# One transformer block and one recurrent/expert block on one core: weight pieces split in pairs, the second mixer in rounds of six column groups, the top-k decode over more pieces

## What is computed

```python
# first block
h = rmsnorm(x, pre_mix_gain);  proj = h @ w_in                # 2048 x 6144
o = 8 heads stick-breaking attention, 8 heads dilated attention with rope, each head normalised
x = x + rmsnorm(o @ w_out)
x = x + rmsnorm(conv_geglu(rmsnorm(x) @ w_up) @ w_down)       # width 5504
# second block
z = rms_norm(x) @ w_in2        # four parts of 1024: xr, gr, gu, gv
xc = depthwise conv of 4 taps over xr
for each direction:            # forward and backward
    a = exp(-8 softplus(-lam) sigmoid(xc @ w_a)); u = sqrt(1 - a*a) * sigmoid(xc @ w_x) * xc
    h_dir = scan(a, u)
a_out = gelu(gr) * (h_forward + h_backward)
b_out = gelu(gu) * (w_s @ layer_norm(gelu(gv)) + b_s)
x = x + concat(a_out, b_out) @ w_out2
# experts: 8 heads, top 16 of 128 + 128 keys, then the top 16 of the 256 sums, of 16384 experts
q = rms_norm(x) @ w_q;  ids, g = topk(topk(q0 @ keys0) + topk(q1 @ keys1))
x = x + (gelu(xn @ expert_u[ids]) * g) @ expert_v[ids]
out = rms_norm(x, final_gain)
```

## Time and profile before

| | us |
|---|---|
| three runs | 3196.59, 3196.71, 3199.45 |
| profiled execution | 3196.1 |
| its span | 3194.8 |
| PE busy | 3073.6 (96%) |
| DVE busy | 2115.2 (66%) |
| ACT busy | 1724.6 (54%) |
| POOL busy | 617.6 (19%) |
| mean granted clock of PE | 0.986 |
| read from HBM | 553.99 MB, 174 GB/s |

### The profile page before, as it was taken

How to read it: one execution, slowest core, us unless ns; L and a number is a source line. 1 busy time by engine, 2 the same in 40 slices (tenths; PEclk the granted TensorE clock), 3 DMA queues, 4 the chain that set the end, 5 groups by cost and what they waited for, 6 DMA issues and landing times.

```text
span 3194.8 us, 52641 instructions
## 1 busy us (share of the span) xinstructions
PE 3073.6 (96%) x21302; PEld 2813.3 (88%) x21302; DVE 2115.2 (66%) x3523; ACT 1724.6 (54%) x3249; POOL 617.6 (19%) x528
## 2 busy tenths in 40 slices
PE   7999989999999999889998999999999999999998
PEld 6999879999998877888897998889998888999886
DVE  5565566666665556665799997557777556777655
ACT  5588755555554445675454544454444454444444
POOL 0011001111110001340233445002326001224200
PEclk9999999999999999999998999999999999999999
DMA  6434435555556554436443445554444555444553
GB/s 243 177 138 146 172 135 184 183 185 185 185 182 216 196 185 178 147 139 222 145 169 137 161 170 176 192 186 172 172 172 172 186 193 175 172 171 173 188 192 135
DMA packets 79875, 559.49 MB, mean 175 GB/s; under 512 B 9361, under 2 KB 10641, under 8 KB 12689
## 3 DMA queue, kind: packets, MB, share of 16 engines
q1 hardware_dynamic: 79632, 556.12, 49.2%
HBM read 553.99 MB, written 2.10 MB: 174 GB/s over the span
## 4 chain that ended last, share of the span: by engine, by line
PE 79%; DVE 4%; ACT 2%; issue 1%; POOL 1%; ACTq 0%; POOLq 0%; DVEq 0%
PE ps L243 14%; PE ps L244 14%; PE ps L245 14%; PE ps L254 12%; PE ps L256 12%; PE ps L255 12%; PE ps L1083 1%; DVE loR L226 1%; PE ps L685 1%; ACT hiR L219 0%; ACT fo L375 0%; DVE lX L783 0%; DVE x L1462 0%; DVE tmp L273 0%; DVE eq L1028 0%
## 5 line engine op out<-in xcount | busy, mean ns | idle before, releaser
L226 DVE TENSOR_TENSOR loR<-raw,hiR 128x512 fp32r<-128x512 f32 x1816 | 1334.5, 739 | 996.2 <-ACT hiR L219 992.8
L219 ACT CAST hiR<-raw 128x512 fp32r<-128x512 f32 x2052 | 1258.5, 619 | 912.7 <-PE ps L256 603.6
L243 PE MATMUL ps<-XAh,hiR 128*128 128x256 f32 x4192 | 1214.1, 290 | 3.1 <-DVE x L1462 2.6
L244 PE MATMUL ps<-XAl,hiR 128*128 128x256 f32 x4192 | 1186.7, 283 | 0.0
L245 PE MATMUL ps<-XAh,loR 128*128 128x256 f32 x4192 | 1186.2, 283 | 0.0
L243 PEld LDWEIGHTS ps<-XAh,hiR 128*128 128x128 f32 x4192 | 804.5, 192 | 6.4 <-DVE x L1462 3.1
L244 PEld LDWEIGHTS ps<-XAl,hiR 128*128 128x128 f32 x4192 | 804.9, 192 | 2.6 <-issue 1.9
L245 PEld LDWEIGHTS ps<-XAh,loR 128*128 128x128 f32 x4192 | 804.4, 192 | 0.0
L226 POOL TENSOR_TENSOR loR<-raw,hiR 128x512 fp32r<-128x512 f32 x236 | 322.5, 1366 | 1413.2 <-ACT hiR L219 1413.2
L254 PE MATMUL ps<-hiR,ah 128*128 128x512 f32 x1024 | 405.2, 396 | 6.2 <-DVE al L1114 6.2
L255 PE MATMUL ps<-loR,ah 128*128 128x512 f32 x1024 | 405.0, 395 | 0.0
(11 more groups left out here) (256 smaller groups left out, 3171.6 us busy)
## 6 DMA issues: line engine op xcount, KB each, us to landing
raw<-in_u_dram SPq DMA_DIRECT2D x128, 1024.0 KB, 4.8
raw<-in_v_dram SPq DMA_DIRECT2D x128, 1024.0 KB, 4.8
raw<-in_w_up_dram SPq DMA_DIRECT2D x86, 1024.0 KB, 4.8
raw<-in_w_down_dram SPq DMA_DIRECT2D x43, 1024.0 KB, 4.8
raw<-in_w_in_qk_dram SPq DMA_DIRECT2D x32, 1024.0 KB, 4.7
raw<-in_w_out_dram SPq DMA_DIRECT2D x32, 1024.0 KB, 4.8
raw<-in_w_in_dram SPq DMA_DIRECT2D x24, 1024.0 KB, 4.8
raw<-in_w_in_v_dram SPq DMA_DIRECT2D x16, 1024.0 KB, 4.8
```

What stands on the lines that cost most here:

```text
L219: e.copy(hiR[:, g % NQ, :], raw[n % NR][:, g % 4, :]).then_inc(S("hi"), 1)
L226: e.tensor_tensor(loR[:, g % NQ, :], raw[g // 4 % NR][:, g % 4, :], hiR[:, g % NQ, :].bitcast(F32), ALU.subtract).then_inc(S("lo_pool" if ...
L243: e.matmul(dst, wh, X.h[:, k, :], start=(k == 0), stop=False)
L244: e.matmul(dst, wh, X.l[:, k, :], start=False, stop=False)
```

## The change

`split_hi` and `split_lo` handle two pieces (128x1024) in one instruction, at even steps only, and wait until both ring places are free; `on_pool` now counts pairs. The second mixer's 24 column groups come in four rounds of six (`xr`, `gr`, `xr`, `gr`, `gu`, `gu`), 24 steps a round, so that the spatial gating of two chunks runs inside each round, in bank 3; the groups share banks 0 to 2. The gate matmuls move from step 20 to 22 of the round, and what follows them by two steps as well. `w_out2` is consumed in the order `WO2_ORDER`. `TKP` becomes 8, `DEC0` 76, the two decodes start 14 steps apart and PE transposes behind their step 13; the gates start at step 106.

The diff, cut to its core:

```diff
+WO2_ORDER = [0, 1, 2, 3, 4, 5, 8, 9, 10, 11, 12, 13, 14, 15, 6, 7]
...
-def on_pool(g):
+def on_pool(u):
+    g = 2 * u
     if P_IN <= g < P_WO2:
-        return g % 6 == 0
+        return u % 6 == 0
     if P_Q <= g < P_U[0]:
...
-            d, p = LO_COUNT[4 * (n - NR) + 3]
+            d, p = LO_COUNT[2 * (n - NR) + 1]
...
     def split_hi(e, g):
-        if g >= NP:
+        if g >= NP or g % 2:
             return
-        n = g // 4
-        if g % 4 == 0:
+        n, r, q = g // 4, g % NQ, g % 4
+        if q == 0:
             e.wait_ge(S(f"raw{n % NR}"), 16 * (n // NR + 1))
         if g >= NQ:
-            e.wait_ge(S("piece"), g - NQ + 1)
-        e.copy(hiR[:, g % NQ, :], raw[n % NR][:, g % 4, :]).then_inc(S("hi"), 1)
+            e.wait_ge(S("piece"), g - NQ + 2)
+        e.copy(hiR[:, r:r + 2, :], raw[n % NR][:, q:q + 2, :]).then_inc(S("hi"), 1)
...
-        if g >= NP or on_pool(g) != pool:
+        if g >= NP or g % 2 or on_pool(g // 2) != pool:
             return
-        e.wait_ge(S("hi"), g + 1)
-        e.tensor_tensor(loR[:, g % NQ, :], raw[g // 4 % NR][:, g % 4, :], hiR[:, g % NQ, :].bitcast(F32),
+        n, r, q = g // 4, g % NQ, g % 4
+        e.wait_ge(S("hi"), g // 2 + 1)
+        e.tensor_tensor(loR[:, r:r + 2, :], raw[n % NR][:, q:q + 2, :], hiR[:, r:r + 2, :].bitcast(F32),
                         ALU.subtract).then_inc(S("lo_pool" if pool else "lo_dve"), 1)
...
     def pe_mixer(e, s):
-        p, d = divmod(s - 20, 16)
+        p, d = divmod(s - 22, 24)
         if d == 0 and 0 <= p < 4:
...
-        c, d = divmod(s - 69, 4)
-        if d == 0 and 0 <= c < 8:
-            b = 4 + c % 2
+        p, d = divmod(s - 21, 24)
+        if d in (0, 4) and 0 <= p < 4:
+            c = 2 * p + d // 4
...
-                e.wait_ge(S("sig"), 32)
-            elif c >= 2:
-                e.wait_ge(S("gm_add"), c - 1)
+            else:
+                e.wait_ge(S("gm_add"), c)
             for tb in range(2):
...
         if d == 0 and 0 <= j < 24:
+            p, v = divmod(j, 6)
             e.wait_ge(S("piece"), P_IN + 4 * j + 4)
-            if j >= 16:
-                e.activation(guT[:, j - 16, :], bank[j % 4][:, 0:T], ACT.Gelu_apprx_tanh).then_inc(S("inev"), 1)
-            elif j % 2:
...
+        p, d = divmod(s - 16, 24)
         if d == 0 and 0 <= p < 4:
             for i in range(2):
                 c = 2 * p + i
-                e.wait_ge(S("inev"), 4 * p + 1 + 2 * i)
...
-            d = s - 16 * p
-            if d == 21:
+            d = s - 24 * p
+            if d == 23:
...
-            elif d == 22:
-                e.wait_ge(S("lam"), 21)
+            elif d == 24:
...
-            elif d == 23:
+            elif d == 25:
...
-            elif d == 24:
...
+            elif d == 26:
...
-            elif d == 26:
+            elif d == 28:
...
-        c, d = divmod(s - 73, 4)
-        if d == 0 and 0 <= c < 8:
+        p, d = divmod(s - 25, 24)
+        if d in (0, 4) and 0 <= p < 4:
+            c = 2 * p + d // 4
             e.wait_ge(S("gm_mul"), c + 1)
             e.copy(XA.h[:, 8 + c, :], gm[c % 2][:, :]).then_inc(S("gm_hi"), 1)
...
-            elif d == 24:
+            elif d == 26:
...
-            elif d in (26, 27):
-                i = d - 26
+            elif d in (28, 29):
+                i = d - 28
...
-        c, d = divmod(s - 70, 4)
-        if d == 0 and 0 <= c < 8:
+        p, d = divmod(s - 22, 24)
+        if d in (0, 4) and 0 <= p < 4:
+            c = 2 * p + d // 4
...
-            elif d in (27, 28):
-                i, c = d - 27, 2 * p + d - 27
+            elif d in (29, 30):
+                i, c = d - 29, 2 * p + d - 29
                 e.wait_ge(S("scan"), 2 * c + 2)
...
-            elif d in (29, 30):
-                c = 2 * p + d - 29
+            elif d in (31, 32):
+                c = 2 * p + d - 31
...
             e.tensor_tensor(gm[c % 2][:, :], gm[c % 2][:, :], guT[:, c, :], ALU.mult).then_inc(S("gm_mul"), 1)
-        c, d = divmod(s - 73, 4)
-        if d == 0 and 0 <= c < 8:
+        p, d = divmod(s - 25, 24)
+        if d in (0, 4) and 0 <= p < 4:
+            c = 2 * p + d // 4
...
-    TK0, TKP = 10, 9
+    TK0, TKP = 10, 8
     DEC0 = TK0 + 8 * TKP + 2
+    DECP = 14
...
-            if s - (DEC0 + 11 * tb) == 10:
+            if s - (DEC0 + DECP * tb) == 13:
...
-            d = s - (DEC0 + 11 * tb)
+            d = s - (DEC0 + DECP * tb)
...
-            elif d == 11:
+            elif d == 14:
...
     def dve_choice(e, s):
-        h, d = divmod(s - TK0, TKP)
         lo8, hi8 = slice(0, 8), slice(8, 16)
         chains = [(0, 0), (0, 1), (1, 0), (1, 1)]
-        if 0 <= h < 8:
+        for h in range(8):
...
+            elif d == 9:
...
-    GATE0 = [DEC0 + 24 - 4 * 16, 1, 1]
+    GATE0 = [DEC0 + 2 * DECP + 2 - 4 * 16, 1, 1]
...
         for j in range(24):
-            if j < 4:
+            if j < 3:
                 e.wait_ge(S("gv"), 2 if j < 2 else 4)
             else:
-                e.wait_ge(S("inev"), j - 3)
+                e.wait_ge(S("inev"), j - 2)
...
-            for k in range(KC):
+            for n, k in enumerate(WO2_ORDER):
                 if fb == 0:
                     e.wait_ge(S("l_lo" if k < 8 else "gm_lo"), k % 8 + 1)
-                moving(e, P_WO2 + 16 * fb + k, XA.h[:, k, :], XA.l[:, k, :], [bank[b][:, :] for b in pair], k == 0,
-                       k == KC - 1)
-                pe_mixer(e, 96 + 16 * fb + k)
+                elif fb == 1 and n == 0:
+                    e.wait_ge(S("gm_add"), 8)
+                moving(e, P_WO2 + 16 * fb + n, XA.h[:, k, :], XA.l[:, k, :], [bank[b][:, :] for b in pair], n == 0,
...
-                if n == P_IN // 4 + 4 * p + 10:
+                if n == P_IN // 4 + 6 * p + 10:
...
-    a["w_out2"] = _mov(I["w_out_2"][0])
+    blocks = []
+    for p in range(4):
+        for c in (2 * p, 2 * p + 1):
+            blocks += [w_in2[:, h * 1024 + c * 128:h * 1024 + (c + 1) * 128] for h in range(2)]
+        blocks += [w_in2[:, 2048 + c * 128:2048 + (c + 1) * 128] for c in (2 * p, 2 * p + 1)]
+    a["w_in2"] = _stat(np.concatenate(blocks, 1))
+    a["w_out2"] = _mov(I["w_out_2"][0], [(fb, k) for fb in range(4) for k in WO2_ORDER])
```

More of the change, by code:

```diff
@@ L50 @@
 NT = NP // 4
-def on_pool(g):
+def on_pool(u):
+    g = 2 * u
     if P_IN <= g < P_WO2:
-        return g % 6 == 0
+        return u % 6 == 0
     if P_Q <= g < P_U[0]:
-        return g % 3 == 0
+        return u % 3 == 0
     for r in range(3):
         if P_U[r] <= g < P_VV[r]:
-            return g % (2 if r == 0 else 3) == 0
+            return u % (2 if r == 0 else 3) == 0
     return False
 LO_COUNT, _n = [], {True: 0, False: 0}
-for _g in range(NP):
-    _n[on_pool(_g)] += 1
+for _u in range(NP // 2):
+    _n[on_pool(_u)] += 1
     LO_COUNT.append((_n[False], _n[True]))
@@ L693, in pe_mixer @@
                 e.wait_ge(S("mix_const"), 64)
-                e.wait_ge(S("sig"), 32)
-            elif c >= 2:
-                e.wait_ge(S("gm_add"), c - 1)
+            else:
+                e.wait_ge(S("gm_add"), c)
             for tb in range(2):
-                m = e.matmul(bank[b][:, half(tb)], gv[:, tb, c * 128:(c + 1) * 128], wsT[:, c, :], start=True,
+                m = e.matmul(bank[3][:, half(tb)], gv[:, tb, c * 128:(c + 1) * 128], wsT[:, c, :], start=True,
                              stop=True)
@@ L704, in act_mixer @@
         if d == 0 and 0 <= j < 24:
+            p, v = divmod(j, 6)
             e.wait_ge(S("piece"), P_IN + 4 * j + 4)
-            if j >= 16:
-                e.activation(guT[:, j - 16, :], bank[j % 4][:, 0:T], ACT.Gelu_apprx_tanh).then_inc(S("inev"), 1)
-            elif j % 2:
-                e.copy(grT[:, j // 2, :], bank[j % 4][:, 0:T]).then_inc(S("inev"), 1)
+            if v >= 4:
+                e.activation(guT[:, 2 * p + v - 4, :], bank[j % 3][:, 0:T], ACT.Gelu_apprx_tanh).then_inc(S("inev"), 1)
+            elif v % 2:
+                e.copy(grT[:, 2 * p + v // 2, :], bank[j % 3][:, 0:T]).then_inc(S("inev"), 1)
             else:
@@ L712, in act_mixer @@
                     e.wait_ge(S("xpz"), 16)
-                e.copy(xp[j // 2][:, 2:258], bank[j % 4][:, 0:T]).then_inc(S("inev"), 1)
-        p, d = divmod(s - 16, 16)
+                e.copy(xp[2 * p + v // 2][:, 2:258], bank[j % 3][:, 0:T]).then_inc(S("inev"), 1)
+        p, d = divmod(s - 16, 24)
         if d == 0 and 0 <= p < 4:
@@ L814, in pool_mixer @@
         for p in range(4):
-            d = s - 16 * p
-            if d == 22:
+            d = s - 24 * p
+            if d == 24:
                 for i in range(2):
@@ L1246, in act_program @@
         e.activation(tmp0[:, 0, :], x[:, 0, :], ACT.Square, accum_out=ss[:, 0:1]).then_inc(S("x0sq"), 1)
-        for g in range(2):
-            split_hi(e, g)
+        split_hi(e, 0)
         e.wait_ge(S("x0sq"), 1)
@@ L1252, in act_program @@
         act_root(e, 0, ss)
-        for g in range(2, 4):
-            split_hi(e, g)
+        split_hi(e, 2)
```

(12 more changed lines are left out.)

56 lines of the change are left out of this document (30 added, 26 removed).

## The result

The changed kernel takes **3211.62 us**, median of six runs (3208.80 to 3215.13); beside them the kernel before took 3197.74 (six runs, 3196.59 to 3199.45). The ratio is 1.0044, with a 95% interval of 1.0031 to 1.0057: slower by 14 us, and by more than the 0.2% that this kernel's measurement can tell. The forecast was 3193.0 within 3171 to 3207, so the result lies outside the range, on the side of rival B. The profiled execution has a span of 3211.5 us, 16.7 more than before.

A forecast was written before the change was run, and what follows sets the result against it. TensorE (PE) was taken as the bound, busy 3073.6 of 3194.8 us, so only its waits and lost clock could move: +8.5 + 2 + 5.4 - 8 - 11 - 0.6 = -3.7, forecast 3193.0 us, range 3171 to 3207.

The forecast's parts named there:

- rival B: Dilated heads: the seven longer waits for `tdl` also cost PE's clock, 1.7 us each, +12, total 3205; chance 0.17.
- Pair splits, price: All stages: a pair takes ACT 1.0 us to its result, DVE 1.14, POOL 2.4; 0.1 saved per pair on each engine.
- Heads: Dilated heads: PE gets `tdl` 1.2 us later, seven times, +8.5 us.
- Rounds: Second mixer: 30.4 us of waits and clock go, new waits of 12.6 and 2.3 and clock of 7.5 come: -8.
- A: Second mixer's rounds: POOL's pair is in time, so 12.6 and 7.5 fall away, total 3173; chance 0.25.
- C: Under the gates: DVE becomes the bound if a POOL pair takes 2.8 us, +7, total 3200; chance 0.10.
- E: Pair splits: pairs are no shorter than two single instructions, total 3196; chance 0.05.
- D: ACT's table switches: a further 1.38 us of drain with each load, by the page, total 3199; chance 0.03.
- Other hand-overs of a head: Dilated heads: hand-overs besides `tdl` lose up to the same but have about that much cover; +2 us.
- Stage borders: Borders at `w_out`, `w_out2` and the ends of `v`: pairs delay evacuations and sums by 0.8 to 1.0 each, together +5.4.
- Top-k and decode: First `fl` wait about 5 us, second decode's wait about 1: -11; gates begin two steps sooner, -0.6.
- The 10.4 us of clock in the old rounds: Second mixer before the change: rounds at 0.92 of full clock over 130 us, 10.4 lost, counted as gain to be had.

The follow-up runs named there:

- longer-wait kernels: The kernel before plus one unused DVE reduction ahead of the rotation in dilated heads 1 to 7, in three lengths (480, 1024, 2048): 3201.17, 3207.39, 3219.34 us.
- e3: The kernel before with only the top-k and decode constants changed (eight steps a head, 14 between the decodes), single splits: 3190.33 us, ratio 0.9979.
- e6: The changed kernel with LA = 5 instead of 6, so that pairs are split at odd steps: 3190.22 us, ratio 0.9977 to the kernel before.

## Why the prediction was wrong, and where it was right

**Right, step by step.** *Pair splits, price*: a cast pair took 1.03 to 1.06 (1.0 to its result forecast), DVE's 1.22 (1.14 to the follower), POOL's 2.34 (2.4). *Worth nothing in a steady stretch*: from 620 to 940 us, `w_up`, where pairs take 20 us off ACT's casts, the stage is 495.4 in both:

```profile
L225 ACT CAST hiR<-raw 128x1024 fp32r<-128x1024 f32 x112 | 117.3, 1047 | 154.3 <-PE ps L252 154.3
```

```profile
L219 ACT CAST hiR<-raw 128x512 fp32r<-128x512 f32 x223 | 137.3, 616 | 63.1 <-PE ps L245 63.1
```

The first line is the changed kernel's, the second the old one's; what ACT saves it adds to its wait for PE. *Heads*: `tdl` 15.2 (near 17), at the place named. *Rounds*: the chain to POOL's pair, and 3.3 three times (4.2); A, the pair in time, is out. C, DVE as the bound under the gates, is out too: under the gates no wait for DVE's `loR` appears, though a gate's product beside a POOL pair now takes 2.60, 0.52 alone, while 1.59 was its blocked time before: DVE stands as long as the pair runs, and there are half as many pairs. The sum over many gates stays (1557 ns a product between 1800 and 1900 us, 1592 before). The product, and POOL's pair beside it, which ends at 1804.86, 0.4 before the product does:

```profile
1802.64 2.60 DVE L1080 TENSOR_TENSOR OG<-OI,selb 128x344 f16<-128x344 f16 x1
1802.40 2.46 POOL L233 TENSOR_TENSOR loR<-raw,hiR 128x1024 fp32r<-128x1024 f32 x1 [3.88 <-ACT hiR L225]
```

E is out by the pair durations, if narrowly on ACT (1.03 to 1.06 for a pair, 1.13 for two in a row). D's term, 1.4 us per switch on top, doesn't appear: in the round the load at 1322.26 takes 1.28 and the function follows 0.01 behind its end (1323.55).

**The step that failed: the heads' clock was priced at nothing.** "PE gets `tdl` 0.3 + 0.38 + 0.53 = 1.2 us later ... **+8.5 us**" ended there, and the clock behind those waits was left to rival B with 0.17. The mechanism of B is what happened, at B's place and nearly B's waits: 4 of 7 waits of 2.17 paid 1.7 each, 6.8 us in q and k, and two more in `w_out` 3.4. Over the whole kernel the forecast's terms hold +0.9 of waits and -4.6 of clock (-10.4 and +7.5 in the rounds, -1.7 in the decode); measured were +2.7 and +14.4. So the waits were forecast nearly right in sum, and 19 of the 20.4 us of the miss are clock: 6.8 in the heads, 5.5 in the rounds, 3.4 at the ends of `v`, 3.3 in `w_out`. My argument against B was that "two of the three paid nothing", and that the seven waits of 1.2 pay nothing. The second half says nothing of waits of 2.2. The first half is a sample of three, one of which did pay: that is a chance of about a third for each wait. The rows also show, which B's text does not say, that the one that paid was the wait of 1.94 and not the longest, of 2.49, so they gave no ground for tying the price to the longest waits. With a chance of a third, the 4 us that B's own text names as the mean should have stood in the sum of the likeliest case, instead of all or nothing. The longer-wait kernels show the cause by itself: the same kind of loss without pairs.

**Terms that were mis-sized**, by stage. *"Other hand-overs of a head ... I add 2"*: 2.6 seen, and 2 of unknown place. *Stage borders*, +5.4: `w_out` took 5.1 for a forecast of 1.8, of which 3.4 is clock, so that its own waits came about as forecast; the wait for `QK` ahead of it grew by 1.9 for a forecast of 0.9. At the ends of `v` the waits for `x` grew by 1.9 and 0.5 where 0.9 each was forecast, and both were followed by half clock, 1.7 each; that the last row of the table is still right (+2.2 for +1.8) is luck, since the last `v` happened to be 2.5 shorter. Together with the heads' clock these two stages miss by 9.1 + 3.3 = 12.4 of the 20.4 by which the profiled executions' difference (+16.7) misses the forecast's -3.7.
*Top-k and decode*, -11 and -0.6: -6.4. The first wait for `fl` fell to 3.1 (5 forecast) and the second is gone; but "its wait goes to about 1" is wrong. In the second decode DVE is busy 21.6 of 23.8 us, and the pair of splits is what comes late:

```profile
1714.60 3.42 DVE L233 TENSOR_TENSOR loR<-raw,hiR 128x1024 fp32r<-128x1024 f32 x1
...
1724.92 2.29 DVE L1038 TENSOR_TENSOR eq<-eq,fl 128x2048 f32<-128x2048 f32 x1
1727.13 1.22 DVE L233 TENSOR_TENSOR loR<-raw,hiR 128x1024 fp32r<-128x1024 f32 x1
```

PE waits 1.0 for the first pair shown and 4.3 for the last. The work that was spread over 14 steps is the same work, and PE only waits for its splits instead of its result. e3 shows the same without pairs (stage 384.6): two waits of 2.0 for DVE's `loR` around the two transposes.
*The 10.4 us of clock in the old rounds* were read from a mean of the granted clock over time. Part of the half-clock time was time in which PE stood still anyway. The kernel before, in the first large wait for `lX` and behind it:

```profile
1318.40:1320.40 2.00, 0.04 (x1) 0.04 (x1) 2.00 (x6) 0.00 (x0) 0.00 (x0) 0.50 0.66 279
1320.40:1325.20 4.80, 4.80 (x11) 3.83 (x12) 0.50 (x1) 1.02 (x3) 0.00 (x0) 0.50 0.60 222
```

Only the second line costs, 4.8 x 0.5 = 2.4. Read so, the three waits lost 6 to 7 us rather than 10.4, and there was less to gain. The 7.5 for the new waits rests partly on the same reading; the three new waits lost 6, but `w_out2` lost 2.9 more than before, most of it behind the wait of 2.9 for `guT`, where nothing was forecast. So the clock of the rounds gave back nothing where 2.9 was forecast. The waits fell by more than forecast, and it is luck that the stages came out at -6.0 for -7.1.

The reason behind the change's loss in one sentence: pairs shorten what is not the bound and delay, at even steps, what is; the delay is 1 us a head, and it lifts seven waits to a length at which PE's clock fell behind four of them.

## What to carry to other kernels

Merging two small instructions of an engine that doesn't bound the kernel saved nothing here, and the merged one delayed what its engine did next at the same count; put it behind the hand-over rather than ahead of it (e6 got 21 us back by moving it one step), or leave it out where hand-overs are dense. A new wait on PE of some 2 us is to be priced at its length plus, by these traces, a chance of about one half of 1.7 us of lost clock (16 of the 28 waits of 2.16 to 2.28 for `tdl`), as its own term in the sum. And lost clock is counted only over time in which PE has work: a mean over a window with waits in it counts the idle time twice.

## What the runs showed of the hardware that was not expected

Seven waits of equal length with the same instructions around them lost clock in 4, 5 or 2 cases (2.17, 2.16, 2.27 us), not in all or none; at 1.15 and 1.71 in none of seven each, and at 3.34 in five. Elsewhere in the kernel one wait of 2.0 lost it in six of eight traces, and one of 2.5 in none of five. POOL's pair blocked DVE for as long as it ran: the 128x344 product took 2.60 us with it and 0.52 alone, so one wider POOL instruction does in one block of 2.1 what two did in blocks of 1.1 each. On all three engines a 128x1024 instruction took 1.7 to 1.8 times the 128x512 one (ACT 1.05 for 0.62, DVE 1.23 for 0.72, POOL 2.34 for 1.28): a merge saves 0.2 us by these means, and 0.1 on ACT against two casts in a row, which took 1.13.
